# Head norms of a two-block transformer: squares split into a rounded part and a rest, projections scaled before the correction

## What is computed

```
def _rms(x, g):
    xf = x.astype(jnp.float32)
    y = xf * lax.rsqrt(jnp.mean(xf * xf, axis=-1, keepdims=True) + EPS)
    return (y * g.astype(jnp.float32)).astype(x.dtype)
...
q = rms_norm(q, q_norm_g) * (HEAD_DIM ** -0.5)
k = rms_norm(k.reshape(bsz, s, N_KV_HEADS, HEAD_DIM), k_norm_g)
```

## Time and profile before

| what | value |
|---|---|
| median of 3 runs | 1452.97 us (1452.92 to 1454.23) |
| the profiled execution's own time | 1451.55 us |
| its span in the trace | 1449.4 us |
| instructions in the span | 19632 |
| PE busy | 1423.9 us (98%) |
| DVE busy | 964.9 us (67%) |
| ACT busy | 627.2 us (43%) |

### The profile page before, as it was taken

One profiled execution on the slowest core, in us unless ns is written; L12 is line 12 of the kernel. 1 busy time (PEld: TensorE's weight loads), 2 busy tenths in 40 slices (PEclk: granted clock), 3 DMA queues, 4 the chain that ended last, 5 costly groups with the idle time before them and its releaser, 6 DMA issues.

```text
span 1449.4 us, 19632 instructions
## 1 busy us (share of the span) xinstructions
PE 1423.9 (98%) x7326; PEld 1172.2 (81%) x7326; DVE 964.9 (67%) x1479; ACT 627.2 (43%) x996; POOL 48.0 (3%) x42
## 2 busy tenths in 40 slices
PE   8999999999999999999999999999899999999999
PEld 6898888888888788888888777777588888888887
DVE  7875777777887577777777767878867433423333
ACT  5634222232356455555544655655544223212221
POOL 0000100001100000000002000000030000000000
PEclk9999999999999999999999999999999999999999
DMA  9985555457623211112202231111022232232222
GB/s 379 336 343 198 181 179 184 180 221 286 266 84 102 87 59 59 59 58 72 74 30 91 70 132 58 64 54 59 30 87 88 90 113 87 89 114 87 89 93 80
DMA packets 35471, 181.55 MB, mean 125 GB/s; under 512 B 4169, under 2 KB 5065, under 8 KB 21074
## 3 DMA queue, kind: packets, MB, share of 16 engines
q1 hardware_dynamic: 33170, 175.75, 33.1%
q10 hardware_dynamic: 2240, 4.98, 1.1%
HBM read 178.07 MB, written 2.11 MB: 124 GB/s over the span
## 4 chain that ended last, share of the span: by engine, by line
PE 82%; DVE 9%; DMA 4%; ACT 2%; issue 2%; SPq 0%; DVEq 0%; ACTq 0%
PE acc L1613 71%; PE norm L1613 4%; PE ada L1613 3%; DMA ada_out<-in_ada 3%; PE turn L1613 2%; DVE w_lo L956 2%; PE turn L2029 1%; DMA ada_v<-in_ada 1%; DVE ada_up L949 1%; PE turn L1892 1%; DVE q_n L949 1%; DVE y_half L949 1%; DVE rstd L949 1%; ACT y L527 1%; DVE s L949 1%
## 5 line engine op out<-in xcount | busy, mean ns | idle before, releaser
L1613 PE MATMUL acc<-h_hi,w_hi 128*128 128x512 f32 x984 | 403.9, 410 | 4.8 <-DVE z_b L1273 3.8
L1613 PE MATMUL acc<-h_hi,w_lo 128*128 128x512 f32 x984 | 384.5, 391 | 0.0
L1613 PE MATMUL acc<-h_lo,w_hi 128*128 128x512 f32 x984 | 383.7, 390 | 0.0
L956 DVE TENSOR_TENSOR w_lo<-w_raw,w_hi 128x2048 fp32r<-128x2048 f32 (+1 forms) x106 | 244.8, 2309 | 67.0 <-ACT w_hi L521 66.8
L521 ACT ACTIVATE w_hi<-w_raw 128x2048 fp32r<-128x2048 f32 (+1 forms) x106 | 200.7, 1893 | 118.6 <-PE acc L1613 117.0
L1613 PEld LDWEIGHTS acc<-h_hi,w_hi 128*128 128x128 f32 x984 | 185.3, 188 | 51.2 <-issue 12.8
L1613 PEld LDWEIGHTS acc<-h_lo,w_hi 128*128 128x128 f32 x984 | 185.4, 188 | 44.2 <-issue 8.4
L1613 PEld LDWEIGHTS acc<-h_hi,w_lo 128*128 128x128 f32 x984 | 184.9, 188 | 39.9
L1613 PE MATMUL acc<-w_hi,h_hi 128*128 128x256 f32 x320 | 93.1, 292 | 3.4 <-DVE w_lo L956 3.4
L1613 PE MATMUL acc<-w_lo,h_hi 128*128 128x256 f32 x320 | 90.8, 285 | 0.0
L1613 PE MATMUL acc<-w_hi,h_lo 128*128 128x256 f32 x320 | 89.8, 284 | 0.0
(11 more groups left out here) (272 smaller groups left out, 2450.8 us busy)
## 6 DMA issues: line engine op xcount, KB each, us to landing
w_raw<-in_weights SPq DMA_DIRECT2D x102, 1024.0 KB, 4.8
ada_v<-in_ada SPq DMA_DIRECT2D x32, 512.0 KB, 6.3
ada_raw<-in_ada SPq DMA_DIRECT2D x32, 512.0 KB, 5.8
ada_out<-in_ada SPq DMA_DIRECT2D x32, 512.0 KB, 6.3
ada_up<-in_ada_first SPq DMA_DIRECT2D x8, 1024.0 KB, 16.8
w_raw<-in_weights SPq DMA_DIRECT2D x4, 768.0 KB, 4.0
x<-in_x SPq DMA_DIRECT2D x2, 1024.0 KB, 6.2
w_first<-in_weights SPq DMA_DIRECT2D x4, 512.0 KB, 13.4
```

What stands on the lines that cost most here:

```text
L956: nc.vector.tensor_tensor(w_lo[par][:, 0:used], w_raw[par][:, 0:used], f32(w_hi[par][:, 0:used]), ALU.subtract)\
L1613: return nc.tensor.matmul(out, lhsT, rhs, start=start, stop=stop)
```

## The change

Each of the 50 sums of squares is done by two float32r matmuls in place of one float32 matmul. ACT now squares twice: once into a float32r tile (`sq_hi`, rounded) and once into `sq`; DVE subtracts the two into a float32r tile (`sq_lo`), and PE adds the products of both with the matrix of ones. The ones are made by GpSimd at the start and are no longer loaded. DVE multiplies the projection by its gain and the first estimate y (`scale_first`, which frees the bank), makes the Newton instruction (`newton`), and multiplies the result by (1.5 - y_half) (`scale_last`). The places of several steps move.

```
+            def square(src, hi, full, bias=0.0):
+                nc.scalar.activation(hi[:, :], src[:, :], ACT.Square, bias=bias)
+                nc.scalar.activation(full[:, :], src[:, :], ACT.Square, bias=bias).then_inc(qsq_ready, 1)
...
+            def square_rest(n, hi, full, lo):
+                dve.wait_ge(qsq_ready, n)
+                nc.vector.tensor_tensor(lo[:, :], full[:, :], f32(hi[:, :]), ALU.subtract).then_inc(qlo_ready, 1)
+            def scale_first(k, out, acc, gain):
+                dve.wait_ge(y0_done, k + 1)
+                return stt(out, acc, gain, y0[:, :], ALU.mult, ALU.mult)
+            def newton(k, count):
+                dve.wait_ge(half_done, k + 1)
+                stt(y0_half[:, :], NB[:, :], count * EPS, y0_half[:, :], ALU.add, ALU.mult).then_inc(newton_done, 1)
+            def scale_last(k, out):
+                dve.wait_ge(newton_done, k + 1)
+                stt(out, y0_half[:, :], 1.5, out, ALU.subtract, ALU.mult, reverse0=True).then_inc(rstd_done, 1)
...
+            def sum_squares(k, n, lhs, hi, lo):
+                pe.wait_ge(qlo_ready, n)
+                pe.wait_ge(newton_done, k)
+                mm(NB[:, :], lhs[:, :], hi[:, :], True, False)
+                mm(NB[:, :], lhs[:, :], lo[:, :], False, True).then_inc(sum_done, 1)
```

In the head loop the sum of squares moves from a quarter of the next piece to its middle, `spread_stats` from behind piece(1) to behind piece(0), and on DVE the order becomes as shown further down:

```
-                    for kts in ((0, 1), range(2, KT)) if mi else (range(4), range(4, KT)):
+                    for kts in (range(4), range(4, KT)):
...
                 if project:
                     piece(0)
-                    piece(1)
...
                 if attend:
                     spread_stats()
                 if project:
+                    piece(1)
                     piece(2)
```

In the rounds of the second block PE's sums move behind unit u's projection, and that of `norm_d` from unit 0 to unit 1. On ACT `rstd_start(norm_d)` moves from unit 0 to unit 1, ahead of `to_hi`; on DVE `diff_norm` moves from unit 1 to unit 2, behind `to_lo`:

```
-                    if project and u in (4, 6, 8):
-                        head_squares(norm2(t, u // 2 - 1), half_ones)
...
-                            if part == 0 and u == 2:
-                                head_squares(norm2(t, 0), half_ones)
                         if u % 2 == 1:
                             last.then_inc(mm_done, 1)
+                        if u in (2, 4, 6, 8):
+                            head_squares(norm2(t, u // 2 - 1), half_r)
...
-                    if a >= 1 and u == 0:
-                        head_squares(norm_d(a - 1), ones)
+                    if a >= 1 and u == 1:
+                        head_squares(norm_d(a - 1), ones_r)
...
+                    if a >= 1 and u == 1:
+                        rest2(norm_d(a - 1))
                     if project and u in (2, 8):
                         to_lo(*divmod(w0 + 1 + u // 4, 2))
-                    if a >= 1 and u == 1:
+                    if a >= 1 and u == 2:
                         diff_norm(a - 1)
+                    if project and u == 2:
+                        rest2(norm2(t, 0))
```

More of the change, by code:

```diff
@@ L495, in _ @@
             nc.gpsimd.memset(idle[:, :].bitcast(F32), 0.0).then_inc(idle_ready, 1)
+            nc.gpsimd.memset(half_r[:, :].bitcast(F32), 0.0).then_inc(half_zeroed, 1)
+            nc.gpsimd.memset(eps_tile[:, :], EPS)
+            nc.gpsimd.memset(ones_r[:, :].bitcast(F32), 1.0).then_inc(ones_ready, 1)
+            pool.wait_ge(half_zeroed, 1)
+            pool.wait_ge(ones_ready, 1)
+            for e in range(2):
+                if e:
+                    pool.wait_ge(half_ready, 1)
+                part = slice(64 * e, 64 * e + 64)
+                nc.gpsimd.memset(half_r[part, part].bitcast(F32), 1.0).then_inc(half_ready, 1)
+            pool.wait_ge(half_ready, 2)
             pool.wait_ge(v_stat_dve, 3)
@@ L663, in _ @@
                 act.wait_ge(acc_freed, 2 * W_KV - 15 + half)
-                nc.scalar.activation(sq[half][:, :], pre[half][:, :], ACT.Square, bias=w_shift[:, half:half + 1]).then_inc(qsq_ready, 1)
-            rstd_start(N_K, NB[:, :], P)
+                square(pre[half], sq_hi_k[half], sq[half], w_shift[:, half:half + 1])
+            rstd_start(N_K, NB[:, :], P, True)
             to_hi(W_KV // 2 + 1, 1)
@@ L677, in _ @@
                             act.wait_ge(mm_done, 4 * u + half + 1)
-                            nc.scalar.activation(sq[half][:, :], G[half][:, :], ACT.Square).then_inc(qsq_ready, 1)
+                            square(G[half], sq_hi_k[half], sq[half])
                     rstd_start(N_K + 2 * c + par, NB[:, :], P)
@@ L795, in head_square @@
                 act.wait_ge(mm_done, 2 * W_Q2 + mi + 1)
-                act.wait_ge(sum_done, k - 1)
-                nc.scalar.activation(sq[k % 2][:, :], bank[:, :], ACT.Square).then_inc(qsq_ready, 1)
-            rstd_start(norm2(0, 0), NB[:, :], 64)
+                act.wait_ge(sum_done, k)
+                square(bank, sq_hi_2, sq[0])
+            rstd_start(norm2(0, 0), NB[:, :], 64, True)
             act.wait_ge(fg_done, 1)
@@ L1035, in h_split @@
                         h_scale(e, kt + 1)
-                    if kt == 4 and between:
-                        between()
+                    if kt in between:
+                        between[kt]()
                     h_rest(e, kt, shift, dilate, h)
@@ L1199, in _ @@
                 rescale(half, G[half][:, :], 2 * W_KV + half + 1, True)
+            dve.wait_ge(bias_ready, 1)
+            for half in range(2):
+                dve.wait_ge(acc_freed, 2 * W_KV - 15 + half)
+                shifted(k_t[:, half, :], pre[half][:, :], w_shift[:, half:half + 1], vecs[:, G_K:G_K + 1], half + 1)
+            for half in range(2):
+                square_rest(half + 1, sq_hi_k[half], sq[half], sq_lo_k[half])
             to_lo(W_KV // 2 + 1, 0)
@@ L1536, in _ @@
             weights2(47)
+            rest2(norm_d(3))
             to_lo(*divmod(W_OUT2 + 1, 2))
@@ L2128, in _ @@
             turn2(47)
-            head_squares(norm_d(3), ones)
+            head_squares(norm_d(3), ones_r)
             values2(46)
```

213 lines of the change are left out of this document (123 added, 90 removed).

## The result

The changed kernel was slower, by 0.3%: 1459.84 us median (1456.63 to 1464.07, 20 runs) against 1456.57 us for the kernel before in the same comparisons (20 runs), ratio 1.0031 with a 95% interval of 1.0018 to 1.0044. On 1456.6 us that is 4.5 us more, 2.6 to 6.4. The forecast had been 3.5 us less.

A forecast was written before the change was run, and what follows sets the result against it. PE was taken to bound the kernel, idle for only 25.5 of 1449.4 us. The terms -14.5 + 0.3 + 0.5 + 0 + 8.3 + 1.0 + 1.0 = -3.4 gave a forecast median of 1449.5 us, range 1441 to 1454.

The forecast's parts named there:

- The head loop: Eight heads: cheaper sums and the waits for z_b and q_n removed, -14.5 us in all.
- that rival: Head loop: bank 0 comes free late, PE waits 1.1 us in each of 8 heads, +8.8, 1458 us; chance 0.08.
- The new wait: Unit 2 of rounds t = 2 and 3: PE waits 4.9 us for the rest; +4.15 a round, +8.3 us.
- t = 1: Second block, round t = 1: DVE's chain binds, so the four cheaper sums save nothing, 0 us.
- t = 0: Second block, round t = 0: gates' work and the first projections' chain cost +0.5 us.
- The rival by which sums save nothing: Whole kernel: weight loads or starts set PE's pace, only the waits go, 1459 us; chance 0.04.
- the step on the clock: Behind the two waits in t = 2 and 3: lower clock costs +1.0 us, bounds 0 and 3.4.
- the base: Whole kernel: profiled execution of 1451.55 us, with the median 1.42 us higher, to which the terms were added.
- The two rivals on that side: Slower side: bank 0 free late, 1458 us, chance 0.08; sums as dear as before, 1459 us, chance 0.04.
- no difference: Rounds t = 2 and 3: wait comes, clock costs 1.7 twice, keys and round 4 cost more; 1453 us, chance 0.18.

The follow-up runs named there:

- r1_fill: Changed kernel plus 14 superfluous 512-column products in PE's wait in unit 2 of rounds t = 2 and 3; 1455.89 us, ratio 1.0000 to the kernel before.
- r2_one_product: Changed kernel with ACT's to_hi earlier, DVE's to_lo later, and one float32 product per sum without rests; 1452.13 us, ratio 0.9973 to the kernel before.
- r2_before_again: The kernel before, unaltered, run again with its trace; 1455.91 us, ratio 1.0007.
- r2_ends: Changed kernel with to_hi earlier, to_lo last in unit 2, but to_lo first at first keys and behind round 4; 1442.93 us, ratio 0.9914 to before.
- r3_block2_one: r2_ends with the 20 sums of the second block done by one float32 product again; 1442.12 us, ratio 0.9915 to the kernel before.

## Why the prediction was wrong

**Right.** The head loop: a head became 1.79 us shorter (from a w_hi at 542.34 to one at 748.46 the lead grows by 10.72 in six heads), 1.81 had been worked out from -14.5 over 8. The whole loop gave 13.1, since in the first heads waits for q_n (0.8), s_b (0.9) and w_lo (0.4) came in. Bank 0 came free in time, so that rival did not occur. The new wait was forecast as 4.9 and was 4.71, with each link in its place, and its own cost, worked out as 8.3 us for the two rounds, was 7.9 (r1_fill). t = 1 changed by -0.1 where 0 had been said, t = 0 by +0.9 where it was +0.5. The rival by which sums save nothing falls with the 0.23 between starts; a head took 1.22 us less for three cheaper sums (r2_one_product against the changed kernel). Against the rule of the Trainium skill on weight loads ("Perfetto Trace Analysis", section "Identifying the Most-Contended Engine"), PE's weight loads were at 81% before and after, while the head loop's time moved with the sums.

**Wrong: the step on the clock.** "The bounds are 0 and 3.4; [...] I take **+1.0**". The rounds t = 2 and t = 3 cost 6.3 and 6.6 us where the wait alone, as laid out, makes 4.15: the clock took 2.2 and 2.4, together 4.6, more than the upper bound. Held against r1_fill, which has the wait and keeps the clock up, it is 5.0 in the first trace, 3.3 in the second, and 5.1 between the medians of 12 runs each. The bound came from the earlier trace rows, where the fall behind thin matmuls costs 1.7 us of work, once for each round. Behind the wait that was the price in one of four cases (0.57 over 4 us); in the other three the lower level lasted about twice as long, 2.9 to 3.4 us of work. I also assumed that DVE's chain would hide part of it. But DVE had run out of work at this point and waited 2.48 us for PE's scores, so most of the slow stretch passed through. The rule of the Trainium skill that I had set beside it ("TensorE: Matmul & The Clock Gate", section "Why this matters for your kernels") is what the trace bears out here; idle gaps between bursts of matmuls do send the clock to its lower level, as all four waits of 4.71 us in the two traces show, and I should have let it choose the upper end. Even the upper end, 2.4 us more, would have left the forecast at 1451.9, so this step alone does not explain the result.

**Wrong as well: the base.** The trace of before that I read had no fall of the clock behind t = 3 nor in the last MLP, and its three runs had a median 3.6 us below that of 20. Both falls are in r2_before_again, 0.79 over 8 us and 0.72 over 6 us, 1.7 us each. In the changed kernel's first trace they were deeper or longer: 0.55 over 6 and 0.57 over 8, 2.7 and 3.4. In its second they were as in r2_before_again, 0.59 over 4 and 0.72 over 6, so the longer ones are not in all its runs. Of the distance from 1449.5 to 1459.84 us, 3.6 us are thus not the change's doing: the forecast was set on a base that three lucky runs gave.

**Left out.** Two things behind t = 3 stood in the forecast at nothing. One is the fall near 1042 us, 1.7 us in both traces of the changed kernel. The other is in the last MLP: from the w_hi that the kernel before has at 1262.71 us to the one at 1429.95 it takes 167.24 us in both its traces, and 168.33 or 168.34 in all eleven traces that have the change, with two products or with one. Seven chunks in a row there, of 48 matmuls of 512 columns each, take 10.98 or 10.99 instead of 10.88 us, with no wait of PE in either trace. That is 1.1 us; its cause stays open.

**The account.** Result and forecast, each against its own base, are 8.0 us apart (+4.5 and -3.5). The first trace has 3.6 of them in t = 2 and 3 (the second 2.0), 1.4 in the head loop, 0.4 in t = 0, at most 1.7 in the fall near 1042 and 1.1 in the last MLP, together 8.2 (6.6). The clock of all the runs points the same way: its mean was 0.9886 over the 20 runs of the changed kernel and 0.9934 over the 12 of r2_before_again, and 0.0048 x 1456 = 7.0 us more of PE's time were lost to it. That is an estimate and an upper one, since not all work lost was time lost: in t = 2 of the first trace 2.9 us of work made 2.2 of time.

**The range.** It gave 0.12 to slower and reached to 1454.0. The two rivals on that side were mishaps in the head loop. The one that decided, the forecast's own wait with its full clock price, was listed as "no difference", 1453, with a bound taken too low and on the low base.

## What to carry to other kernels

When a step is moved, look at what stands behind it on its own engine and how long the thing is: three short instructions ahead of a chunk's rounding (1.9 us, and 2.3 on the next engine) held up a product that did not need the chunk. Price a wait of the matmul engine as the wait plus the slow stretch behind it; here a wait of 4.7 us stood for 4.0 us of a round, and the clock behind it added 1.3 to 2.6. Make each sum cheaper only where the engine that does it binds: in the head loop the 0.39 us a sum came through in full (0.41), in the second block no gain was seen.

## What the runs showed that I had not expected

Fourteen products for nothing in each of two waits made the kernel 5.1 us faster, as the clock stayed at 1.00 behind them instead of 0.51 for 6 us. And the spread between runs of one unchanged kernel on one core goes with the clock: 1451.11 us at a mean of 0.997, 1460.86 us at 0.989. The best versions, r2_ends and r3_block2_one, are at 0.9914 and 0.9915 of the kernel before.
